# A hybrid decoder block on one core: the last expert batch's down matrices by column halves, and one pair of loads moved behind another

## The reference, cut to what matters

```python
y = jnp.zeros((B * L, D), dtype=F32)
for e in range(N_EXPERTS):                                   # 32
    h = jax.nn.silu(xt @ w_gate[e]) * (xt @ w_up[e])         # gate, up: 1024 x 256
    y = y + combine[:, e:e + 1] * (h @ w_down[e])            # down: 256 x 1024
...
h = rms_norm(h, final_norm_w)                                # h * rsqrt(mean(h*h) + eps) * w
return h[:, N_META:]
```

## Time and profile before

| what | us |
|---|---|
| median of 3 runs (lowest, highest) | 710.31 (709.94, 710.39) |
| the profiled execution | 712.34 |
| its span, first to last instruction | 710.4 |
| TensorE busy in matmuls | 619.9 (87%) |
| VectorE busy | 316.0 (44%) |
| ScalarE busy | 245.7 (35%) |

### The profile page before, as it was taken

One profiled execution on the slowest core, in us unless ns is written; L12 is line 12 of the kernel. 1 busy time (PEld: TensorE's weight loads), 2 busy tenths in 40 slices (PEclk: granted clock), 3 DMA queues, 4 the chain that ended last, 5 costly groups with the idle time before them and its releaser, 6 DMA issues.

```text
span 710.4 us, 13896 instructions
## 1 busy us (share of the span) xinstructions
PE 619.9 (87%) x5701; PEld 508.3 (72%) x5701; DVE 316.0 (44%) x718; ACT 245.7 (35%) x570; POOL 36.9 (5%) x92
## 2 busy tenths in 40 slices
PE   2799999899999999999999899997887956859575
PEld 2799999798998889998889799875544514425141
DVE  3534348899978657453524374124211111101112
ACT  4424547667777444235112951113100100001002
POOL 8000000000000001100210100000000000000000
PEclk9989999999999999999999999998999979789896
DMA  9925552332333432301224186995999999999981
GB/s 292 294 86 178 178 171 71 116 119 67 113 120 119 124 115 67 96 20 28 63 91 135 45 273 189 419 421 218 353 420 420 421 421 423 421 422 421 421 351 60
DMA packets 69692, 155.96 MB, mean 220 GB/s; under 512 B 7171, under 2 KB 56437, under 8 KB 57349
## 3 DMA queue, kind: packets, MB, share of 16 engines
q1 hardware_dynamic: 65792, 154.36, 58.3%
q10 hardware_dynamic: 3844, 0.82, 0.6%
HBM read 154.12 MB, written 1.05 MB: 218 GB/s over the span
## 4 chain that ended last, share of the span: by engine, by line
PE 69%; DMA 19%; DVE 5%; ACT 3%; issue 2%; SPq 0%; DVEq 0%; ACTq 0%
PE bank L755 31%; DMA arena<-in_expert_w_down_dram 18%; PE bank L1154 6%; PE bank L924 5%; PE bank L737 4%; PE bank L744 4%; PE bank L902 3%; PE bank L1135 2%; PE bank L867 2%; PE bank L844 2%; PE bank L1120 1%; PE bank L1161 1%; DVE w_lo L286 1%; PE bank L812 1%; DMA arena<-in_meta_tokens_dram 1%
## 5 line engine op out<-in xcount | busy, mean ns | idle before, releaser
L755 PE MATMUL bank<-uT_hi,w_hi 128*128 128x272 f32 (+1 forms) x576 | 177.1, 308 | 7.0 <-issue 4.2
L755 PE MATMUL bank<-uT_lo,w_hi 128*128 128x272 f32 (+1 forms) x576 | 166.6, 289 | 0.0
L755 PE MATMUL bank<-uT_hi,w_lo 128*128 128x272 f32 (+1 forms) x576 | 166.6, 289 | 0.0
L286 DVE TENSOR_TENSOR w_lo<-arena,w_hi 128x1024 fp32r<-128x1024 f32 x80 | 98.8, 1239 | 55.2 <-ACT w_hi L281 54.9
L755 PEld LDWEIGHTS bank<-uT_hi,w_hi 128*128 128x128 f32 x576 | 111.4, 193 | 10.2 <-issue 5.1
L755 PEld LDWEIGHTS bank<-uT_lo,w_hi 128*128 128x128 f32 x576 | 111.7, 194 | 1.6 <-issue 0.5
L755 PEld LDWEIGHTS bank<-uT_hi,w_lo 128*128 128x128 f32 x576 | 111.3, 193 | 0.0
L281 ACT ACTIVATE w_hi<-arena 128x1024 fp32r<-128x1024 f32 x80 | 83.7, 1052 | 4.4 <-PE bank L755 4.2
L1154 PE MATMUL bank<-arena 128*32 128x512 f32 x256 | 42.7, 827 | 37.1 <-DMA arena<-in_expert_w_down_dram 36.0
L1135 PE MATMUL bank<-arena 128*32 128x256 f32 x1024 | 56.9, 380 | 0.0
L1154 PEld LDWEIGHTS bank<-arena 128*32 128x32 f32 x256 | 10.7, 144 | 62.8 <-issue 61.3
(11 more groups left out here) (316 smaller groups left out, 835.9 us busy)
## 6 DMA issues: line engine op xcount, KB each, us to landing
arena<-in_w_in_dram SPq DMA_DIRECT2D x36, 1024.0 KB, 5.4
arena<-in_expert_w_gate_dram SPq DMA_DIRECT2D x32, 1024.0 KB, 23.9
arena<-in_expert_w_up_dram SPq DMA_DIRECT2D x32, 1024.0 KB, 24.0
arena<-in_expert_w_down_dram SPq DMA_DIRECT2D x32, 1024.0 KB, 21.2
arena<-in_w_branch_attn_dram SPq DMA_DIRECT2D x4, 1024.0 KB, 5.1
arena<-in_w_branch_dn_dram SPq DMA_DIRECT2D x4, 1024.0 KB, 7.2
arena<-in_w_out_dram SPq DMA_DIRECT2D x4, 1024.0 KB, 6.5
arena<-in_x_dram SPq DMA_DIRECT2D x4, 512.0 KB, 4.7
```

What stands on the lines that cost most here:

```text
L286: nc.vector.tensor_tensor(w_lo[q % NSPLIT], src, w_hi[q % NSPLIT].bitcast(F32), ALU.subtract).then_inc(w_lo_ready, 1)
L755: last = pe.matmul(ps[:, 0:b.shape[2]], a[:, c, :], b[:, c, :], start=(c == 0 and i == 0), stop=(c == NC - 1 and i == 2))
```

## The change

The eighth batch's down matrices come in as column halves: first the left 512 columns of all four, then the right 512, with one semaphore (`last_in`) for the four right halves. The down matmuls of the left half are followed at once by their combine matmuls, and only then by the down matmuls of the right half. In the seventh batch's loads, slots 0 and 1 of the eighth batch are issued behind the shared slots 10 and 11 instead of ahead of their wait. TensorE's last pair of batches is written out as straight code. The last norm is rearranged: squares of the left half are taken as soon as it is combined, VectorE weighs three of the four banks before the root is known and scales token tile 0 afterwards in one instruction out of SBUF, ScalarE scales one half of token tile 1. The squares' unused output goes to `osq2` in place of `junk`.

```diff
-            def load_batch(first_expert, odd, used, first=False, last=False):
+            def load_last(first_expert, used):
+
+                for half in range(2):
+                    cols = slice(half * 512, (half + 1) * 512)
+                    for e in range(EPB):
+                        if half == 0 and e == [i for i in range(EPB) if NC + i not in TWINS][0]:
+                            sp.wait_ge(down_used, 2 * used + 2)
+                        signal = last_in if half else twin_in[NC + e] if NC + e in TWINS else slot_in[NC + e]
+                        sp.dma_start(down_of(e, True)[:, :, cols],
+                                     w_down_c[:, first_expert + e, :, cols]).then_inc(signal, 16)
+
+            def load_batch(first_expert, odd, used, first=False, last=False, next_to_last=False):
...
+                if last:
+                    load_last(first_expert, used)
+                    return
                 if not first:
                     load_twins(first_expert, odd, range(NC, SLOTS))
-                if not last:
+                if not next_to_last:
                     load_twins(first_expert + EPB, not odd, range(2))
                 sp.wait_ge(down_used, 2 * used + 2)
                 load_shared(first_expert, odd, range(NC, SLOTS))
+                if next_to_last:
+                    load_twins(first_expert + EPB, not odd, range(2))
...
             for t in range(TT):
                 sp.wait_ge(out_ready, t + 1)
+                if t:
+                    sp.wait_ge(out_a, 1)
...
+            def combine_half(b, half):
+
+                pe.wait_ge(down_d if half else down_a, b + 1)
+                for t in range(TT):
+                    last = pe.matmul(bank[2 * t + half][:, :], pickT[:, t, :], dsb[:, half * 512:(half + 1) * 512],
+                                     start=False, stop=False, skip_group_check=True)
+                    if half == 0 and t == TT - 1 or half == 1 and t == 0:
+                        last.then_inc(half_sum, 1)
+                if half:
+                    last.then_inc(combined, 1)
...
                 for half in range(2):
+                    if last_one and half:
+                        combine_half(b, 0)
+                        pe.wait_ge(last_in, 16 * EPB)
...
                     last.then_inc(down_used, 1)
+                if last_one:
+                    combine_half(b, 1)
+                    return
...
-            with pe.Fori(1, N_BATCH // 2) as pair:
+            with pe.Fori(1, N_BATCH // 2 - 1) as pair:
                 for odd in range(2):
                     batch(pair, odd)
+            batch(N_BATCH // 2 - 1, 0)
+            batch(N_BATCH // 2 - 1, 1, last_one=True)
...
+            act.wait_ge(half_sum, 1)
+            for t in range(TT):
+                last = squares(t, 0)
+            last.then_inc(ssq3_ready, 1)
+            act.wait_ge(half_sum, 2)
+            squares(0, 1).then_inc(ssq3_ready, 1)
             act.wait_ge(combined, N_BATCH)
...
+            squares(1, 1).then_inc(ssq3_ready, 1)
             for t in range(TT):
                 act.wait_ge(var3_ready, t + 1)
                 root(rstd, rstd3_ready, ssq, t)
+            act.wait_ge(rstd3_ready, TT)
+            act.wait_ge(weighted, 1)
+            act.activation(result[:, 1, 0:512], result[:, 1, 0:512], ACT.Copy, scale=rstd[:, 1:2]).then_inc(out_a, 1)
...
+            dve.wait_ge(ssq3_ready, 1)
+            mark(weigh(0, 0))
+            weigh(1, 0).then_inc(weighted, 1)
+            variance(0)
+            mark(weigh(0, 1))
+            variance(1)
+            follow()
+            dve.wait_ge(rstd3_ready, 1)
+            ts(result[:, 0, :], result[:, 0, :], rstd[:, 0:1], None, ALU.mult).then_inc(out_ready, 1)
+            dve.wait_ge(rstd3_ready, 2)
+            stt(result[:, 1, cols[1]], bank[3][:, :], rstd[:, 1:2], fnorm_b[:, cols[1]], ALU.mult, ALU.mult).then_inc(out_ready, 1)
```

More of the change, by code:

```diff
@@ L209, in hybrid_block @@
         gate_up_twin = [at(yaT_start, 2, UNIT), at(after_experts, 2, UNIT), at(u2_start - 2 * UNIT, 2, UNIT)]
-        result = at(yaT_start, TT, D)
+        result, osq2 = at(yaT_start, TT, D), at(u2_start - 2 * UNIT, TT, D)
         assert u2_start - 2 * UNIT >= uT_start + TT * D + NC * 36 and u2_start + TT * D + UNIT + 36 + NC <= yaT_start
@@ L249, in hybrid_block @@
         ssq3_ready, var3_ready, rstd3_ready, out_ready = sem("ssq3_ready"), sem("var3_ready"), sem("rstd3_ready"), sem("out_ready")
+        weighted, out_a = sem("weighted"), sem("out_a")
+        last_in, half_sum = sem("last_in"), sem("half_sum")
         w_in_v = w_in[0].rearrange("(c p) n -> p c n", p=P)
@@ L257, in hybrid_block @@
         w_down_r = expert_w_down[0].rearrange("e (p c) n -> p e (c n)", c=2)
+        w_down_c = expert_w_down[0].rearrange("e (p c) n -> p e c n", c=2)
         w_down_e = expert_w_down[0].rearrange("e (c p) n -> p e c n", p=P)
@@ L551, in _ @@
                 load_batch((2 * pair + 3) * EPB, True, 2 * pair + 2)
-            load_batch((N_BATCH - 2) * EPB, False, N_BATCH - 3)
+            load_batch((N_BATCH - 2) * EPB, False, N_BATCH - 3, next_to_last=True)
             load_batch((N_BATCH - 1) * EPB, True, N_BATCH - 2, last=True)
@@ L1112, in wait_weights, with batch @@
                     pe.wait_ge(slot_in[s], pair * 16 + before + 16)
-            def batch(pair, odd, first=False):
+            def combine_half(b, half):
[7 more added lines that the diff above has]
+                    last.then_inc(combined, 1)
+            def batch(pair, odd, first=False, last_one=False):
                 b = 2 * pair + odd
@@ L1531, in _, with squares @@
             act.preload_act_table_set("natural_log_exp_and_others")
-            act.wait_ge(combined, N_BATCH)
[L1533 to L1539, removed]
+            def squares(t, half):
+                return act.activation(osq2[:, t, half * 512:(half + 1) * 512], bank[2 * t + half][:, :], ACT.Square,
+                                      accum_out=sc[:, 8 + half, t:t + 1])
+            act.wait_ge(half_sum, 1)
[4 more added lines that the diff above has]
+            squares(0, 1).then_inc(ssq3_ready, 1)
+            act.wait_ge(combined, N_BATCH)
+            squares(1, 1).then_inc(ssq3_ready, 1)
             for t in range(TT):
@@ L2030, in _, with weigh, variance @@
                 dve.wait_ge(f_sum, N_EXPERTS * 4 + 1)
-            for t in range(TT):
-                dve.wait_ge(ssq3_ready, t + 1)
+            cols = [slice(half * 512, (half + 1) * 512) for half in range(2)]
+            def weigh(t, half):
+                return tt(result[:, t, cols[half]], bank[2 * t + half][:, :], fnorm_b[:, cols[half]], ALU.mult)
+            def variance(t):
+                dve.wait_ge(ssq3_ready, t + 2)
                 link(tt(ssq[:, t:t + 1], sc[:, 8, t:t + 1], sc[:, 9, t:t + 1], ALU.add))
                 ts(ssq[:, t:t + 1], ssq[:, t:t + 1], 1.0 / D, EPS, ALU.mult, ALU.add).then_inc(var3_ready, 1)
[L2037 to L2042, removed]
+            dve.wait_ge(ssq3_ready, 1)
[9 more added lines that the diff above has]
+            stt(result[:, 1, cols[1]], bank[3][:, :], rstd[:, 1:2], fnorm_b[:, cols[1]], ALU.mult, ALU.mult).then_inc(out_ready, 1)
 _INS = ['x', 'meta_tokens', 'norm1_w', 'w_in', 'lambda_q1', 'lambda_k1', 'lambda_q2', 'lambda_k2', 'da_subln_w',
```

## The result

The changed kernel took 706.72 us (median of 9 runs, 705.45 to 707.80) against 710.12 us (median of 9, 708.93 to 711.06): a ratio of 0.9949, 95% interval 0.9936 to 0.9961. The forecast was 706.5 in 703.8 to 708.8. The profiled execution of the changed kernel took 707.71.

A forecast was written before the change was run, and what follows sets the result against it. Expert-weight transfers bound the kernel to about 691 us, then the work left after the last bytes. Last batch -1.6 (cold start of 2.3 included) and tail -2.2 make -3.8 on 710.31: 706.5 us, range 703.8 to 708.8.

The forecast's parts named there:

- The transfers: Weight queue: seventh batch's downs start at 661.6, slot 6 still lands at 678.9, right halves at 692.2 (386 GB/s).
- The 512 B rule: Last down matrices: smallest transfer still at line rate is 512 B, by which the halves would land at 691.3.
- Rival C: Slow 2 KB pieces delay the last combine; no gain if right halves land at 699.4 (233 GB/s); chance 0.04.
- The cold start before the gates: TensorE idles 4.8 to 6.5 us before the eighth batch's gates; gate and up stage costs +2.3 us (1.6 to 2.9).
- The last batch: TensorE from the gates at 679.06 to the last combine's end at 700.0, against 701.64: -1.6 us.
- The tail: From the last combine's end to the span's end: 6.6 us against 8.8, so -2.2 us (bounds -1.4, -2.7).
- Rival A: TensorE's clock holds through the idle time before slot 6; 2.3 us come back, 704.2 us; chance 0.16.
- Rival D: Unrolled last two batches stall on instruction fetches: 1 to 3 us, 708 to 709.5; 0.17 shared with partial rival B.
- rival B: Clock falls before the last downs and stays low: up to 7.3 us more, 713.8 us; chance 0.05 in full.
- the lesser form: Last batch only partly cold: one more cold start of 2.3 to 2.9 us, 709 us; 0.17 shared with Rival D.

The follow-up runs named there:

- e2: Kernel before with only the move of the eighth batch's first pair in the queue: 706.76 us, ratio 0.9957.
- e8: The changed kernel run again, unaltered: 706.55 us, ratio 0.9950.
- e5: Changed kernel with four extra unused matmuls in TensorE's idle time before the last gates: 706.54 us, ratio 0.9946.
- e4: Changed kernel without the column halves, move and new norm kept: 706.79 us, ratio 0.9948.
- e1: Changed kernel with the eighth batch's first pair back in its old place, halves and new norm kept: 705.62 us, ratio 0.9942.
- e10: Same program as e1, run again: 705.87 us, ratio 0.9928.
- e7: Halves alone: e1 with the old norm put back, pair unmoved: 708.21 us, ratio 0.9972.
- e6: Kernel before with new norm and written-out last batches, plus two extra unused matmuls before the last downs: 706.70 us, ratio 0.9947.
- e9: e1 with one extra unused matmul in the last batch's wait for `hid`: 704.99 us, ratio 0.9917.
- e11: Changed kernel with four extra matmuls before the last gates and one in the wait for `hid`: 704.24 us, ratio 0.9910.

## Why the prediction was right, and where it was off

**The transfers.** Right. The seventh batch's downs started at 661.51 (forecast 661.6) and the last gates waited for slot 6 until 678.92 (679.06). SP's later issue of the pair cost nothing: the DMA rate from 672 to 679 was 420 GB/s, 421 before. The estimate of 386 GB/s for 2 KB pieces, interpolated between the rates of 1 KB and 8 KB, was met by 386 in the trace, and it is the pieces and not the stage: with 8 KB pieces e2 moved 418 to 434 GB/s in the slices from 681 to 685. The right halves were in about 1 us before the forecast 692.2, since the 2 KB pieces were moving in the slice at 680 already (361 GB/s) and not from 681.4 on. The 512 B rule of the Trainium skill (page "DMA: Bandwidth & Descriptors", Specifications) would have had 421 for the 2 KB pieces. Rival C fell with that: no wait for the right halves in any chain here.

**The cold start before the gates.** Right in place and sign. It was charged with 2.3 us and measured 1.7 (8.80 against 7.11), 2.0 in e8. e5 shows the cause: with TensorE kept busy, the gates take 7.11 us. All four profiles with the move and no extra matmuls have the cold start: 8.80 and 9.08 in the changed kernel, 8.80 in e2, 9.08 in e4. This agrees with the page "TensorE: Matmul & The Clock Gate" (Part 1) of the Trainium skill, that the throttled state is the default. What was said to follow from it, that the halves are better without the move, held in e1's profile (200.8 against 202.7 by F) and not in e10's (203.5). In the medians the kernel without the move gains 4.2 and 4.9 us (e1, e10), the changed one 3.4 and 3.9, with intervals that overlap: leaving the move out is as good and perhaps better.

**The last batch.** Measured from the gates' start to T: 699.69 - 678.92 = 20.8 us, forecast 20.9. The cold start was 0.6 shorter, the two half-combines 1.98 each rather than 1.83, the rest within 0.1. Relative to F the whole gained 1.45 us (196.40 against 197.86), forecast 1.6.

**The tail.** 6.3 us instead of 8.8, a gain of 2.45, forecast 2.2. The scaling out of SBUF took 0.75 us, so the row with 0.73 was the right one of the two. VectorE left its loop in 0.60 us and not 0.47, but started the scaling 1.16 us behind T where 1.5 was forecast, because its copy ended 2.03 us ahead of T and not 1.85 (the right combine is longer) and the steps behind the loop came out 0.25 us shorter. The working has small slips: VectorE's terms add up to T + 1.39 and not 1.47, the bounds to 705.3 and 707.9, and of the DMA line's slices only 29 to 38 are at 9; none of them changes the forecast. By F the sum of both is -3.9 us; forecast -3.8.

**The rivals.** Rival A (the clock holds before the gates) didn't occur in either profile of the changed kernel. Rival D didn't either: the last gates start 175.6 and 175.2 us behind F in the changed kernel and 175.2 in e2, which keeps the loop. Of rival B the lesser form, one more cold start of 2.3 to 2.9 us between the up matmuls and the last downs, is real: it happened in e5, e7 and e10. What the prediction said against it, that the same gap before 524.36 left the clock up, did not hold in those three, so that its forecast stayed clear of this cold start was in part luck. Both profiles of the changed kernel escaped it though they have the same gap (2.69 us from 687.72 to 690.41). In them the gates ended later, and the clock had come back only 5 us before their end. Whether the cold gates protect what follows or only shift it in time, these runs don't settle; they show that a gap which left the clock up in one execution let it fall in another of the same program.

**What the prediction did not see.** It took the change to be worth the early left half plus the shorter tail, less a cold start, and had no price for each part by itself. The accounting of the whole was right, but the runs apart tell another story: the last batch's 2.9 us of cold downs, which the kernel before pays on the critical path, is the largest prize. The move takes it alone (e2), the halves take it by starting the downs earlier (e1), two wasted matmuls take it as well (e6), and it can be had only once: with the move in place, e4 without the halves is level with the changed kernel. So parts that are worth 3.05 (move), 2.2 (halves) and 0.7 us (norm) alone in the medians give 3.4 to 3.9 together and not 6. The other way round, halves and norm help each other: 4.2 and 4.9 us without the move.

## What to carry to other kernels

Look at TensorE's clock at the point where the last data lands. Idle time ahead of it is paid for behind it, at half speed; either put the idle time elsewhere, where another transfer covers the slow work, or fill it with matmuls that write to a free bank. When several edits each remove the same cold start, test them one by one, since the sum counts it only once. And compare executions from a common event near the change (here the first batch's down stage) as well as by their whole time, when the work ahead of it varies by more than the change is worth.

## What was unexpected of the hardware

A gap that had not cooled the clock in the first two batches (downs of 3.64 and 3.68 us in the kernel before) did so in the last one: 2.7 us between the end of the up matmuls and the downs, with 0.9 us of transposes in it. In e10, e5 and e7 the clock then fell about 1 us into the following work, while TensorE was busy, and the left combine ran at 3.78 us. The same program (e1) also ran it at 1.98. With one extra matmul of 0.91 us in that gap both profiles (e9, e11) stayed warm, and the medians of e5 and e11 bear it out. What sets whether the clock falls in the gap without it is open.

The clock's fall is not tied to the moment at which TensorE stops. Behind TensorE's last work it came after 2.1 us in e8, after 2.2 us in the kernel before (at 690.5), and after 5.2 us in the first profile of the changed kernel and 5.4 in e2, where the gates had already begun.

The start of the expert stage varied by 2.7 us between profiles (501.08 to 503.80) though nothing ahead of it differs. The two profiles of the changed kernel are 2.3 us apart in span, and 2.2 of that lies ahead of F; their critical chains are 1.9 us apart already at 43 us. Between e1 and e10 it is the other way round: 2.3 us in span, all of it and more behind F, from the clock. I have not traced the early part further.
